# Which queue issues the weight loads: a transformer encoder on one core

## The chip, the cores and the metric

One core of a Trainium2 chip runs the whole kernel. The metric is the device time of one execution in microseconds (us); the kernel before took 2937.95 us, the median of three runs (2937.46 to 2938.80).

The core's engines work side by side and meet through semaphores: TensorE (PE in the profile, PEld its weight loads), VectorE (DVE), ScalarE (ACT), GpSimd (POOL) and SyncE (SP). SP computes nothing: it issues DMA transfers. GpSimd issues DMAs too. Each of the two works through its own list in order, so an instruction that waits holds back those behind it. SP's transfers stand in the profile under queue q1 (hardware_dynamic), GpSimd's under q0 (software_dynamic).

## What is computed

```python
for l in range(2):                                   # 1024 tokens, width 1024, fp32
    h = rms_norm(x, g_mix[l]); proj = h @ w_in[l]
    # A: 6 heads, dense, from a latent space; B: 6 heads, dilated windows; C: 4 heads, 2-D neighbourhood
    qa  = rms_norm(c_q,  q_norm[l])  @ w_uq[l]       # up-projection of the latents
    kva = rms_norm(c_kv, kv_norm[l]) @ w_ukv[l]
    mixed = concat(rms_norm(o_a), rms_norm(o_b), rms_norm(o_c))
    x = x + mixed @ w_out[l]
    h2 = rms_norm(x, g_mlp[l])
    x = x + square(relu(h2 @ w_mlp_in[l])) @ w_mlp_out[l]
return rms_norm(x, g_final)
```

## The kernel before

Tokens are cut into ST = 8 tiles of 128. Every fp32 matrix is split into a high part and the rest, and three matmuls replace one: high by high, high by low, low by high. ACT writes the high part (`split_job`, `split_a`, `hi_up`, `hi_down`), DVE the rest (`rest`, L891).

**Weights** come as units of up to 2048 fp32 numbers per partition (1 MB) in a stream in HBM. A layer has NU = 50 units: two for each of nine jobs (a, bq, up, bk, bv, cqk, cv, o0, o1), then 32 for the feed-forward part. They go through two buffers, `raw[0]` for even and `raw[1]` for odd units. A load adds to `raw_in`; ACT waits for that and copies the high part; DVE then takes the low part and adds to `split_lo`. A load of unit u waits for `split_lo` of unit u - 2 (`load_unit`), since only then its buffer is free. In all there are 102 loads, every one on SP's list.

**Stages of a layer.** (1) Norm of x, tile by tile: ACT squares and sums (L661) and takes the root (L664), DVE scales by it and by the gain gB (L908), TensorE transposes (L1201), ACT and DVE write high and low parts of hT. Each tile's ACT part waits for DVE's part of the tile before. x is parked in HBM, as its place is used for staging. (2) Projections, in the order of the list `EVENTS`, which all engines follow: entries "acc" (the 24, 18 or 6 matmuls of a tile, L1233, four PSUM banks in turn), "turn" (transposes of a staged tile, L1270, high and low parts into `tst`, L777 and L767 on ACT) and "split" (a weight unit). Queries and keys go to HBM as features (`feats`, stored from one of NTS = 3 slots of `tst`, by SP), values as `values` (from one of two slots of `vst`, by GpSimd, L614). ACT waits, before it fills a slot, for the stores that left it. (3) Attention, 16 heads in turn; SP loads features, values and biases, GpSimd the values of the C heads and moves their outputs. (4) Norm, output projection o0 and o1, x back from HBM. (5) Norm and feed-forward part: 16 groups, each an "up" half (L1407) and a "down" half (L1422), one unit each, loaded in a hardware loop (L560).

**SP's list** in order: the rows of x with ident, gB and, after x tiles 3 and 5, the units 0 and 1 (L395); pair, cos, sin. In each layer: gL, units 2 and 3, the park stores of x (L496), gB, units 4 and 5, then `EVENTS`: at each "split" the load of unit u + 2 (L406), at each turn to be stored its feature stores (L515 for "ur", L521 and L526 for "cqk", L532 for the others); then heads; x back, with units 16 and 17 after tile 1; gB; the loop over 32 units; gB; units 0 and 1 of the next layer; the stores of the output.

**GpSimd's list:** memsets (eps is one, L575; ACT waits for it before its first table load), and in each layer the 24 value stores in the order of `EVENTS`, each after DVE's low part; then the C heads' transfers (L587, L597, L605).

Of the kernel before, what the change touches and what calls it, by code (L numbers as in the profile page):

```python
# [52 lines left out]
def unit_len(job, half):  # L53
    if job == "up":
        return (2 * UQ, UKV)[half]
    return KT // 2 * WIDTH[job]
# [162 lines left out]
def encoder(nc, x_in, wstream, gains, lat_gains, cos_in, sin_in, bias_b, bias_c, ident_in, pair_in, out):  # L219
# [69 lines left out]
    with ctx:  # L289
# [43 lines left out]
        def hold(eng):  # L333

            eng.sem_inc(passed, 1)
# [5 lines left out]
        def unit_of(job, half):  # L341
            return 2 * JOBS.index(job) + half
# [42 lines left out]
        def _(sp):  # L385
# [4 lines left out]
            for t in range(1, ST):  # L390
                sp.dma_start(x[:, t, :], x_in[t * P:(t + 1) * P, :]).then_inc(x_loaded[t], 16)
                if t in (3, 5):
                    u = t // 2 - 1
                    length = unit_len("a", u)
                    sp.dma_start(raw[:, u, 0:length], wstream[u, :, 0:length]).then_inc(raw_in[u], 16)  # L395
            sp.dma_start(pair[:, :], pair_in).then_inc(const_in, 16)
            sp.dma_start(cos[:, :, :], cos_in).then_inc(const_in, 16)
            sp.dma_start(sin[:, :, :], sin_in).then_inc(const_in, 16)
            for k in range(2):
                sp.sem_inc(fin_out[k], 16 * (ST // 2))  # L400

            def load_unit(l, u, length=ULEN):

                sp.wait_ge(split_lo, l * NU + u + 1)
                hold(sp)
                sp.dma_start(raw[:, u % 2, 0:length], wstream[l * NU + u, :, 0:length]).then_inc(raw_in[u % 2], 16)  # L406

# [81 lines left out]
            for l in range(DEPTH):  # L489
                sp.dma_start(gL[:, :], lat_gains[l]).then_inc(gl_in, 16)  # L490
                for u in (2, 3):
                    load_unit(l, u, unit_len(JOBS[u // 2], u % 2))

                for t in range(ST):
                    sp.wait_ge(hn_ready, l * N_HN + t + 1)
                    sp.dma_start(x_park[t], x[:, t, :]).then_inc(parked, 16)  # L496
                load_gain(l, 1)
                for u in (4, 5):
                    load_unit(l, u, unit_len(JOBS[u // 2], u % 2))
                turn = vt = 0  # L500
                for e in EVENTS:
                    if e[0] == "acc" and e[1] == "cv":
                        first_head(l, e[2], turn, vt)
                    if e[0] == "split":
                        u = unit_of(e[1], e[2]) + 2
                        load_unit(l, u, unit_len(JOBS[u // 2], u % 2))
                    elif e in STORED:
                        n = TURNS.index(e)
# [39 lines left out]
                for t in range(ST):  # L548
                    sp.wait_ge(hn_ready, l * N_HN + ST + t + 1)
                    sp.dma_start(x[:, t, :], x_park[t]).then_inc(x_loaded[t], 16)  # L550
                    if t == 1:
                        load_unit(l, 16)
                        load_unit(l, 17)
                load_gain(l, 2)
                with sp.Fori(0, NG) as g:
                    load_unit_pair = l * NU + MLP0 + 2 * g
                    for k in range(2):
                        sp.wait_ge(split_lo, load_unit_pair + k + 1)
                        hold(sp)
                        sp.dma_start(raw[:, k, :], wstream[l * NU + MLP0 + 2 * g + k]).then_inc(raw_in[k], 16)  # L560

                load_gain(l, 3)
                for u in range(2):
                    load_unit(l, NU + u, unit_len("a", u))
                for t in range(ST):
# [7 lines left out]
        def _(pool):  # L573

            pool.memset(eps[:, :], EPS).then_inc(eps_set, 1)  # L575

            def load_grid_values(l, n):
# [30 lines left out]
            for l in range(DEPTH):  # L608
                for vt, e in enumerate(VSTAGED):
                    k = vt % 2  # L610
# [19 lines left out]
                park_grid(l, grids[-1])  # L630
                read_grid(l, grids[-1])


# [943 lines left out]
```

## Time and profile before

| | us |
|---|---|
| median of three runs | 2937.95 |
| the profiled execution | 2937.11 |
| its span, first to last instruction | 2935.0 |
| TensorE matmul busy (97%) | 2854.4 |
| VectorE busy (59%) | 1719.8 |
| ScalarE busy (36%) | 1058.0 |
| GpSimd busy (5%) | 141.7 |

Busy times are sums over an engine's instructions; matmuls are pipelined, so their sum says how long TensorE had work, not that it ran at its peak. The span is cut by stages: projections of layer 0 to about 287 us, attention to 650, output projection to 763, feed-forward to 1476; then the same for layer 1. q1 carried 254.16 MB, q0 29.41 MB. An idle stretch of an engine is printed in brackets with what ended it: the "releaser". A releaser with q (DVEq, ACTq) is that engine's sequencer, mostly a semaphore after a drain.

### The profile page before, as it was taken

How to read it: one execution, taken by the hardware profiler on the slowest of the kernel's cores; microseconds unless marked ns; L12 is line 12 of the kernel's file. 1: busy time of each engine (PE TensorE's matmuls, PEld its weight loads, DVE VectorE, ACT ScalarE, POOL GpSimd, SP SyncE). 2: the span in 40 equal slices, each digit the busy share in tenths (PEclk: the TensorE clock that was granted, in tenths of full speed). 3: DMA queues.
4: the chain of work that ended last, by engine and by line, in shares of the span. 5: the costliest groups of instructions: out<-in, count | busy, mean ns of one | idle time of the engine just before them, and what ended most of it. 6: DMA issues, size and time to landing. Idle time of an engine off the chain costs nothing.

```text
span 2935.0 us, 39902 instructions
## 1 busy us (share of the span) xinstructions
PE 2854.4 (97%) x14640; PEld 2439.2 (83%) x14640; DVE 1719.8 (59%) x2998; ACT 1058.0 (36%) x1976; POOL 141.7 (5%) x253
## 2 busy tenths in 40 slices
PE   7999999989999999999999999999899999999998
PEld 7898888878888888888798978888788888888887
DVE  5641777875555455455666337788655455455457
ACT  5332777874311111111244237778632111111113
POOL 0000330000000000000000012300000000000000
PEclk9999999999999999999999999999999999999999
DMA  5656884313111111111146577743221111111111
GB/s 195 183 188 156 199 192 113 88 43 115 43 44 57 43 43 57 43 43 64 45 176 205 168 191 179 178 101 87 67 78 43 43 57 43 43 57 43 43 62 69
DMA packets 182359, 285.34 MB, mean 97 GB/s; under 512 B 48848, under 2 KB 138576, under 8 KB 172496
## 3 DMA queue, kind: packets, MB, share of 16 engines
q1 hardware_dynamic: 171600, 254.16, 29.7%
q0 software_dynamic: 10624, 29.41, 3.6%
q8 instruction: 81, 1.33, 0.2%
q14 instruction: 54, 0.44, 0.1%
HBM read 210.60 MB, written 72.88 MB: 97 GB/s over the span
## 4 chain that ended last, share of the span: by engine, by line
PE 86%; DVE 5%; issue 3%; DMA 3%; ACT 2%; DVEq 1%; SPq 0%; ACTq 0%; POOLq 0%
PE ps L1407 24%; PE ps L1233 20%; PE ps L1422 18%; PE ps L1306 7%; PE ps L1320 6%; PE ps L1352 6%; PE ps L1362 2%; PE ps L1201 1%; DMA biasC<-in_bias_c 1%; DMA values<-vst 1%; PE ps L1270 1%; PE ps L1345 1%; DVE x L1154 1%; DVE hn L908 1%; DVE vbuf L1141 1%
## 5 line engine op out<-in xcount | busy, mean ns | idle before, releaser
L1422 PE MATMUL ps<-w_dn,hid 128*128 128x512 f32 x3072 | 713.6, 391 | 1.4
L1407 PE MATMUL ps<-hT,w_up 128*128 128x512 f32 x3072 | 702.5, 389 | 3.3 <-DVE hT L891 3.3
L1422 PEld LDWEIGHTS ps<-w_dn,hid 128*128 128x128 f32 x3072 | 573.6, 188 | 132.5 <-DVE x L1154 14.0
L1407 PEld LDWEIGHTS ps<-hT,w_up 128*128 128x128 f32 x3072 | 576.2, 188 | 123.1 <-ACT rbuf L841 3.7
L1233 PE MATMUL ps<-ws,hT 128*128 128x384 f32 (+3 forms) x3072 | 607.7, 356 | 3.1 <-issue 1.6
L1233 PEld LDWEIGHTS ps<-ws,hT 128*128 128x128 f32 x3072 | 535.1, 190 | 50.3 <-DVE ws L891 2.7
L1154 DVE TENSOR_TENSOR x<-ps,x 128x512 f32<-128x512 f32 x512 | 342.9, 689 | 223.9 <-PE ps L1422 223.7
L1141 DVE TENSOR_TENSOR vbuf<-rbuf 128x512 f32<-128x512 f32 x128 | 88.6, 692 | 371.0 <-ACT rbuf L841 371.0
L792 ACT ACTIVATE pT<-ps 128x512 fp32r<-128x512 f32 (+1 forms) x448 | 240.5, 582 | 141.5 <-PE ps L1320 139.6
L891 DVE TENSOR_TENSOR pT<-ps,pT 128x512 fp32r<-128x512 f32 (+1 forms) x448 | 281.4, 664 | 6.9 <-ACT pT L792 5.8
L841 ACT ACTIVATE rbuf<-ps 128x512 f32<-128x512 f32 x128 | 76.6, 598 | 553.9 <-PE ps L1407 553.9
L799 ACT ACTIVATE prob<-ps,a_nm 128x1024 f32<-128x1024 f32 (+1 forms) x256 | 252.8, 987 | 35.5 <-DVE a_nm L1056 16.2
L827 ACT ACTIVATE w_dn<-raw 128x2048 fp32r<-128x2048 f32 x32 | 61.3, 1917 | 556.3 <-PE ps L1422 556.3
L1320 PE MATMUL ps<-ident,prob 128*128 128x128 f32 x1728 | 232.2, 273 | 5.9 <-DVE pT L891 3.0
L1306 PE MATMUL ps<-head 128*128 128x512 f32 x768 | 229.6, 400 | 7.1 <-DVEq L1002 5.2
L1320 PEld LDWEIGHTS ps<-ident,prob 128*128 128x128 f32 x1728 | 202.7, 140 | 39.2 <-ACT prob L799 8.3
L1352 PE MATMUL ps<-pT,head 128*128 128x512 f32 x768 | 225.2, 416 | 1.8 <-DVE pT L891 1.8
L1306 PEld LDWEIGHTS ps<-head 128*128 128x128 f32 x768 | 140.4, 190 | 37.1 <-DVEq L1002 6.1
L1352 PEld LDWEIGHTS ps<-pT,head 128*128 128x128 f32 x768 | 131.1, 190 | 20.8 <-DVE pT L891 4.0
L1039 DVE TENSOR_REDUCE a_nm<-ps 128x1 f32<-128x1024 f32 x96 | 117.4, 1223 | 51.1 <-PE ps L1306 48.9
L1044 DVE CUSTOM_DVE_ANT_0 ps<-ps,tabB 128x1024 f32<-128x1024 f32 x96 | 118.1, 1230 | 37.8 <-PE ps L1306 35.8
L1201 PE MATMUL ps<-ident,hn 128*128 128x128 f32 x448 | 70.3, 307 | 40.8 <-DVEq L910 20.5
(85 smaller groups left out, 2140.8 us busy)
## 6 DMA issues: line engine op xcount, KB each, us to landing
raw<-in_wstream SPq DMA_DIRECT2D x76, 1024.0 KB, 4.9
head<-feats SPq DMA_DIRECT2D x192, 256.0 KB, 6.3
feats<-tst SPq DMA_DIRECT2D x128, 192.0 KB, 2.6
values<-vst POOLq DMA_DIRECT2D x32, 384.0 KB, 3.2
head<-values SPq DMA_DIRECT2D x24, 512.0 KB, 4.0
biasC<-in_bias_c SPq DMA_DIRECT2D x16, 768.0 KB, 12.3
raw<-in_wstream SPq DMA_DIRECT2D x12, 768.0 KB, 5.8
x_park<-x SPq DMA_DIRECT2D x16, 512.0 KB, 9.5
```

Of the source, the lines that this page charges most:

```text
L792: act.activation(pT[:, b % 2, HI, k0:k0 + nk, (it % 4) * P:(it % 4 + 1) * P], ps[:, 4 + g % 2, 0:nk * P].rearrange("p (k s) -> p k s", s=P ...
L799: act.activation(probability(i), score(i), ACT.Exp, bias=a_nm[:, i:i + 1], scale=-1.0 if ITEMS[i][0] == "B" else 1.0, accum_out=a_den[:, i ...
L891: return dve.tensor_tensor(out_lo, full, words(hi), ALU.subtract)
L1044: dve.tensor_tensor_reduce(out=score(i), in0=score(i), in1=tabB[:, 896 - P * q:896 - P * q + SEQ], scale=1.0, scalar=-NEG, op0=ALU.add, op ...
L1141: dve.tensor_tensor(vbuf[:, k % 2, :], rbuf[:, k % 2, :], rbuf[:, k % 2, :], ALU.mult)
L1154: dve.tensor_tensor(x[:, s, cols], ps[:, 2 + m % 4, :], x[:, s, cols], ALU.add)\
L1233: last = pe.matmul(out_, a, b, start=(n == 0), stop=(n == len(mms) - 1))
L1306: last = pe.matmul(ps[:, b0 + kh, :], a, b, start=(k == 0), stop=(k == len(mm) - 1))
L1320: last = pe.transpose(ps[:, 4 + g % 2, j * P:(j + 1) * P], probability(i)[:, c:c + P], ident[:, :])
L1352: last = pe.matmul(bank, hb[:, 4096 + kt * P:4096 + (kt + 1) * P], pT[:, b % 2, w, kt, :], start=(part == 0 and kt == 0 and w == 0), stop= ...
L1407: last = pe.matmul(ps[:, k % 2, :], w_up[0 if first else 1][:, w1, kt, ft * P:(ft + 1) * P], hT[:, w2, kt, sh * 512:(sh + 1) * 512], start ...
L1422: last = pe.matmul(ps[:, 2 + m % 4, :], hid[slot][:, w1, ft, s * P:(s + 1) * P], w_dn[1 if last_group else 0][:, w2, ft, nh * 512:(nh + 1) ...
```

## The change

All weight loads leave SP's list and go to GpSimd's, with their waits. SP keeps x, features, head loads, biases, gains, constants and outputs. GpSimd starts with units 0 and 1, ahead of the memset of eps; in each layer it loads units 2 to 5, then walks `EVENTS`: at a "split" it loads unit u + 2, at a value tile it stores the values. After the C heads it loads units 16 and 17, then runs the loop over the 32 feed-forward units, then the next layer's units 0 and 1.

```diff
@@ sync
             for t in range(1, ST):
                 sp.dma_start(x[:, t, :], x_in[t * P:(t + 1) * P, :]).then_inc(x_loaded[t], 16)
-                if t in (3, 5):
-                    u = t // 2 - 1
-                    length = unit_len("a", u)
-                    sp.dma_start(raw[:, u, 0:length], wstream[u, :, 0:length]).then_inc(raw_in[u], 16)
...
-                for u in (2, 3):
-                    load_unit(l, u, unit_len(JOBS[u // 2], u % 2))
...
-                for u in (4, 5):
-                    load_unit(l, u, unit_len(JOBS[u // 2], u % 2))
...
-                    if e[0] == "split":
-                        u = unit_of(e[1], e[2]) + 2
-                        load_unit(l, u, unit_len(JOBS[u // 2], u % 2))
-                    elif e in STORED:
+                    if e in STORED:
...
-                    if t == 1:
-                        load_unit(l, 16)
-                        load_unit(l, 17)
                 load_gain(l, 2)
-                with sp.Fori(0, NG) as g:
...
                 load_gain(l, 3)
-                for u in range(2):
-                    load_unit(l, NU + u, unit_len("a", u))
@@ gpsimd
+            for u in range(2):
+                length = unit_len("a", u)
+                pool.dma_start(raw[:, u, 0:length], wstream[u, :, 0:length]).then_inc(raw_in[u], 16)
             pool.memset(eps[:, :], EPS).then_inc(eps_set, 1)
+
+            def load_unit(l, u, length=ULEN):
+
+                pool.wait_ge(split_lo, l * NU + u + 1)
+                hold(pool)
+                pool.dma_start(raw[:, u % 2, 0:length], wstream[l * NU + u, :, 0:length]).then_inc(raw_in[u % 2], 16)
...
             for l in range(DEPTH):
-                for vt, e in enumerate(VSTAGED):
+                for u in range(2, 6):
+                    load_unit(l, u, unit_len(JOBS[u // 2], u % 2))
+                for e in EVENTS:
+                    if e[0] == "split":
+                        u = unit_of(e[1], e[2]) + 2
+                        load_unit(l, u, unit_len(JOBS[u // 2], u % 2))
+                    if e not in VSTAGED:
+                        continue
+                    vt = VSTAGED.index(e)
                     k = vt % 2
                     pool.wait_ge(acc_free_dve, l * DVE_FREE_N + frees_before(ACCS.index(e) + 1, False))
...
                 read_grid(l, grids[-1])
+                for u in (16, 17):
+                    load_unit(l, u)
+                with pool.Fori(0, NG) as g:
+                    load_unit_pair = l * NU + MLP0 + 2 * g
+                    for k in range(2):
+                        pool.wait_ge(split_lo, load_unit_pair + k + 1)
+                        hold(pool)
+                        pool.dma_start(raw[:, k, :], wstream[l * NU + MLP0 + 2 * g + k]).then_inc(raw_in[k], 16)
+                for u in range(2):
+                    load_unit(l, NU + u, unit_len("a", u))
```

## Rows read from the trace of the kernel before

**Rows 1.** The page, busy us, share of the span and instructions.

```profile
PE 2854.4 (97%) x14640; PEld 2439.2 (83%) x14640; DVE 1719.8 (59%) x2998; ACT 1058.0 (36%) x1976; POOL 141.7 (5%) x253
```

**Rows 2.** Timeline of PE: start, us, instruction [idle before it <-releaser].

```profile
7.73 1.94 PE L1201 MATMUL ps<-ident,hn 128*128 128x128 f32 x8 [7.73 <-DVEq L910]
...
118.73 0.69 PE L1270 MATMUL ps<-ident,stage 128*128 128x128 f32 x2 [2.72 <-DVE tst L891]
...
125.57 0.52 PE L1270 MATMUL ps<-ident,stage 128*128 128x128 f32 x3 [2.42 <-ACTq L735]
...
129.27 2.36 PE L1233 MATMUL ps<-ws,hT 128*128 128x384 f32 x12 [0.77 <-DVE ws L891]
...
1571.95 0.52 PE L1270 MATMUL ps<-ident,stage 128*128 128x128 f32 x3 [1.67 <-ACTq L735]
...
1575.65 2.36 PE L1233 MATMUL ps<-ws,hT 128*128 128x384 f32 x12 [0.75 <-DVE ws L891]
```

**Rows 3.** The tile raw: who waited, us, times; then its loads' landing.

```profile
  ACT ws L647: 1.1, 2
...
DMA to landing us min/median/max: 3.6/4.9/12.6
```

**Rows 4.** Timeline of SP's queue, the start.

```profile
3.63 0.45 SPq L395 DMA_DIRECT2D raw<-in_wstream  x1
...
24.51 8.70 SPq L406 DMA_DIRECT2D raw<-in_wstream  x2
```

**Rows 5.** Timeline of ACT, the start.

```profile
4.45 1.06 ACT L661 ACTIVATE hn<-x 128x1024 f32<-128x1024 f32 x1 [2.21 <-DMA x<-in_x]
...
7.92 1.06 ACT L661 ACTIVATE hn<-x 128x1024 f32<-128x1024 f32 x1 [1.96 <-DMA x<-in_x]
...
11.14 1.06 ACT L661 ACTIVATE hn<-x 128x1024 f32<-128x1024 f32 x1 [0.73 <-DVEq L910]
```

**Rows 6.** Windows: us, busy us by engine, granted clock, DMA share, GB/s.

```profile
4.00:6.00 2.00, 0.00 (x0) 0.00 (x0) 0.00 (x0) 1.44 (x3) 0.00 (x0) 1.00 1.02 367
...
14.00:16.00 2.00, 0.84 (x4) 0.87 (x5) 1.53 (x4) 1.85 (x4) 0.00 (x0) 1.00 1.02 428
```

**Rows 7.** GpSimd's value stores: ns min/median/max; us from issue to landing.

```profile
L614 POOL DMA_DIRECT2D values<-vst x48: 542/542/738, 107.0 to 1736.9; - x48
...
DMA to landing us min/median/max: 2.6/3.3/8.2
```

**Rows 8.** The two DMA queues in 277.5 to 279.1 us: packets, MB, share.

```profile
q1 hardware_dynamic: 98, 0.33, 64.8%
q0 software_dynamic: 70, 0.22, 39.9%
```

**Rows 9.** The chain that ended last: start, us, piece; then page's DMA issues.

```profile
119.11 5.13 DMA feats<-tst
...
1566.12 4.50 DMA feats<-tst
...
feats<-tst SPq DMA_DIRECT2D x128, 192.0 KB, 2.6
```

**Rows 10.** Timeline of SP's queue before the first of these stores.

```profile
116.82 0.35 SPq L406 DMA_DIRECT2D raw<-in_wstream  x1
118.70 4.33 SPq L532 DMA_DIRECT2D feats<-tst  x6
```

**Rows 11.** Windows at the two stores (columns as in rows 6).

```profile
120.00:122.00 2.00, 2.00 (x10) 2.00 (x9) 0.06 (x1) 0.00 (x0) 0.00 (x0) 0.63 0.90 310
...
1565.00:1569.00 4.00, 3.26 (x12) 3.25 (x13) 2.05 (x5) 1.36 (x3) 0.00 (x0) 0.57 0.99 287
```

**Rows 12.** Timelines of SP's queue and ACT in the value projection.

```profile
195.78 2.55 SPq L406 DMA_DIRECT2D raw<-in_wstream  x2
...
204.18 0.49 ACT L743 ACTIVATE vst<-ps 128x384 fp32r<-128x384 f32 x1 [4.29 <-DMA values<-vst]
```

**Rows 13.** Timelines of ACT and SP's queue, a group of the feed-forward part.

```profile
1008.30 1.92 ACT L827 ACTIVATE w_dn<-raw 128x2048 fp32r<-128x2048 f32 x1 [19.86 <-PE ps L1422]
...
1012.78 22.48 SPq L560 DMA_DIRECT2D raw<-in_wstream  x2
```

More of the change, by code:

```diff
@@ L400, in _ @@
                 sp.sem_inc(fin_out[k], 16 * (ST // 2))
[L402 to L406, printed above, removed]
             def load_gain(l, k):
@@ L550, in _ @@
                     sp.dma_start(x[:, t, :], x_park[t]).then_inc(x_loaded[t], 16)
-                    if t == 1:
-                        load_unit(l, 16)
-                        load_unit(l, 17)
                 load_gain(l, 2)
-                with sp.Fori(0, NG) as g:
[L556 to L560, printed above, removed]
                 load_gain(l, 3)
-                for u in range(2):
-                    load_unit(l, NU + u, unit_len("a", u))
                 for t in range(ST):
```

## Prediction

> **What bounds the kernel now.** I read the busy times first. TensorE's matmuls cover 97% of the span, and VectorE, the next, 59% [rows 1]. So the change can gain or lose only where TensorE stands still for something a transfer delivers. Next I read its timeline for pauses, in order of time. Two places matter here [rows 2]. At the start it waits 7.73 us for its first operand, and shorter times before the next five sets of transposes. In the latent up-projection of layer 0 it pauses 2.72, 2.42 and 0.77 us near 118 to 129 us; layer 1 has the same three, the last two at 1571.95 and 1575.65 us with 1.67 and 0.75 us. The feed-forward stage, where 64 of the 102 weight loads are, has no pause that a weight load ends.
>
> The list of who waited for the tile `raw` says the same from the other side: of all the converting copies that read it, ACT waited for the transfer twice, 1.1 us in all [rows 3]. Loading weights sooner is thus worth nothing by itself. What the change can alter is what travels beside the weights: the rows of x at the start, the feature stores (which lose the weights ahead of them in SP's queue) and the value stores (which get them ahead in GpSimd's).
>
> **The start.** Now SP issues x tile 0, the identity, gB, x tiles 1 to 3, weight unit 0, x 4 and 5, unit 1, x 6 and 7 [rows 4]. ACT waits 2.21 us for x tile 0 and starts at 4.45, waits 1.96 us for tile 1 and starts at 7.92; from then on it waits for DVE, not for a transfer: tile 2 follows at 11.14, 3.2 us on [rows 5]. That is a serial chain (ACT's square and root, DVE's scaling, ACT again), so what x tile 1 loses, everything behind it loses. From 4 to 16 us the DMA engines are full, at 367 GB/s in the first 2 us slice of that and 428 in the last [rows 6].
>
> After the change GpSimd issues both units, 832 KB each (1.70 MB), as its first work. It has nothing before them but the memsets of the first microsecond, and a DMA costs it 0.54 us, its first one 0.74 [rows 7]. The bytes then run beside SP's queue from about 2.3 us, as SP's own first bytes do. How two queues share the engines shows in one window, where the value store on GpSimd's queue and 4 KB rows on SP's were both moving: 70 packets of one and 98 of the other, shares of 39.9% and 64.8% [rows 8]. Neither had the way to itself. Up to tile 1's landing SP's queue carries x 0, 64 KB, gB and x 1, 1.64 MB, about as much as the two units. If the queues alternate row by row, the 16 rows per engine of the two units are all served before the 24 rows per engine of x 0, gB and x 1 are done. Tile 1 then lands later by the whole time of the units: 1.70 MB at 410 GB/s (my estimate between the slices of [rows 6]) = 4.1 us. It would land near 12.0 instead of 7.9. Tile 0 would slip by about 2 us and gB, which DVE needs for tile 0, to about 10.4; both lie inside the same 4.1 us, since tile 1 would come no sooner than that anyway. Tiles 2 to 7 were needed at 11.14 and later and now have 4.1 us more; their bytes end where they ended before, near 20 us. The delayed memset of eps (1.3 us) only moves ACT's table load, which lies in the 2.21 us wait. Bounds: zero if SP's queue were served first or GpSimd's first DMA came late, 4.1 at the top, because there are no more bytes to be overtaken by. I take **+4.1**, the end that the near-equal shares of the shared window speak for. Nothing later gives this back: from its first projection to 118 us TensorE has no pause to absorb it.
>
> Two edits on SP's list go with it. Park stores of x no longer wait behind units 2 and 3 (24.51 for the first of the two [rows 4]); they go out earlier, and TensorE runs through that stretch, so this is worth 0. Those units come no later than now.
>
> **The feature stores.** In both layers the chain of the end runs through one feature store: issued at 118.70 it lands after 5.13 us, and in layer 1 after 4.50 us, while the median of such stores is 2.6 [rows 9]. SP had issued a 768 KB weight load 1.9 us before it (116.82 [rows 10]; layer 1 has the same order). In one queue the store waits for the rest of it. With the load in GpSimd's queue the store starts at once but shares: I estimate that it is done about 1 us sooner. Bounds: nothing (the DMA engines are nearly full there, 0.90 and 0.99 busy [rows 11], and the same bytes must move), and 2.5 and 1.9 us if the store took its median. ACT waits for that store, TensorE for ACT (the 2.42 and 1.67 us pauses), so it is on the path. I take **-1.0 in each layer, -2.0 in all**. The 2.72 us pause ahead of it is set by ACT's and DVE's order of work and stays. Later waits for feature stores repeat with no load near them and stay.
>
> **What GpSimd's queue takes on.** Each load but the first two waits for a low half that DVE writes in the order of the same list as the value stores, so no store is held by a load's wait; a load's issue costs a store 0.5 us. The one tight spot is the value projection: units of cv are loaded at 195.78, and ACT, whose copy at 204.18 needs the third value store landed, waited 4.29 us for it already [rows 12]. Queued behind 2 x 512 KB it may land 1 to 2 us later. But that copy frees one of four banks, and TensorE, which takes 2.36 us for half a tile of 24 matmuls [rows 2], wants it back three tiles on, 12 us or more later: 0. In the feed-forward loop a load leaves at 1012.78, and its buffer, read at 1008.30 [rows 13], is read again one group later, near 1052 (two loads, one for each half of a group, span 22.48 us from the first's start to the second's end, so a group takes some 44 us); landing takes 4.9 us [rows 3], so some 34 us of cover. It covers GpSimd's issue, its loop and any wait of GpSimd for DVE: 0. At the layers' joint the next bq units come sooner, and with that the 1.1 us that ACT waited for them [rows 3]; TensorE is not waiting there: 0. Units 16 and 17 no longer follow x's first two reloads: 0.
>
> **Clock.** TensorE's granted clock fell to half for short stretches after pauses (0.63 of full in 120 to 122 us, 0.57 in 1565 to 1569 us [rows 11]). A shift of 4 us can move such a stretch onto more or fewer matmuls. TensorE was busy all 2.0 us of the first at 0.63, where 1.3 us of full clock would have done, so one such shift is worth about 1 us either way; with a handful of places I allow 2 us each way, centred on 0.
>
> **Sum.** The profiled run took 2937.11 us for a span of 2935.0, 0.84 under the median of the three runs. On the run: 2937.11 + 4.1 - 2.0 = 2939.2. On the median: 2937.95 + 2.1 = **2940.0**.
>
> **Rivals.**
> *Only the order changes, no store gets faster.* The DMA engines are full around the two stores, so the weight bytes may delay a store as much from a second queue as from the same one. Then only the start counts: 2937.95 + 4.1 = 2942.0. For it: the busy share of 0.90 to 0.99; against: the load was issued first and its bytes stand wholly ahead now. The Trainium skill, page "DMA: Bandwidth & Descriptors", section "Issuing engines are not separate DMA queues", says that transfers started on several engines run on the same 16 DMA engines and that spreading them saves only the time of issuing. By that rule this rival is the outcome; the long landings behind a weight load speak against it, as a queue's order seems to count there.
>
> *The start costs nothing.* GpSimd's first DMA is slow to begin, or SP's queue goes first. Then x tile 1 lands as before and only the stores gain: 2936.0. For it: no row shows how long GpSimd's first DMA takes to begin; against: value stores of 384 KB land in 2.6 us at best, issue to end [rows 7], and there are over 5 us before tile 1 is in.
>
> *The pauses vanish whole.* If the stores take their median and the half-clock stretch goes as well, each layer saves up to 2.42 + 0.77 and 1.67 + 0.75 us plus 1 us of clock, 7.6 in all; with no loss at the start 2930.4.
>
> *Slower: value stores stall behind weights.* Place: the eight value stores of the bv projection in each layer, with two staging buffers, behind the cqk and cv units in one queue. The price starts when a store lands more than about 12 us late, for then ACT cannot free a bank in time. A value store that did wait among other traffic took 8.2 us at most [rows 7]. If GpSimd's queue moved 1 MB in 15 us and not in 3 (70 GB/s), one stall of 5 us per layer would follow: 2937.95 + 4.1 + 10 = 2952. A value store of 384 KB that lands 2.6 us after its issue moved at 150 GB/s or more, so I hold it unlikely.
>
> **Chances.** Forecast 0.50; no store gain 0.20; no start cost 0.15; pauses vanish whole 0.05; slower by stalls 0.07; none of these 0.03. What this kernel's measurement can tell from no change is about 0.2%, 5.9 us: under 2932.1 or over 2943.8. Faster is the case of the vanished pauses and a bit: 0.06. Slower is the stall case and the top end of the first two with the clock against them (+4.1 + 2): 0.14. Same: 0.80. The range takes the first three cases with 1 to 2 us of clock on either side and a little of the slow tail: 2934.5 to 2945.0.
>
> **What would show each step.** Start: ACT's square of x tile 1 at about 12.0 instead of 7.92, tile 0's near 6.4, all that follows later by as much. Stores: landing of the chain's store at 4 instead of 5.13 us, TensorE's pause of 2.42 down to about 1.4. GpSimd: 102 DMAs more, of some 0.55 us each. Feed-forward: same pauses as before. I would be wrong if x tile 1 kept its time, if a pause on raw or on vst appeared in TensorE's list, or if the feed-forward's pace of 44 us per group changed.

## The result

| | median us (lowest to highest) | runs |
|---|---|---|
| before | 2938.99 (2935.04 to 2943.01) | 20 |
| after | 2943.39 (2939.32 to 2946.27) | 20 |

The ratio after to before is 1.0015, with a 95% interval of 1.0008 to 1.0021: slower by 4.4 us, between 2.4 and 6.2. The forecast of 2940.0 lay 3.4 us under the median, its range held it, and the change is within the 0.2% that was called "same"; but the interval leaves no doubt about the sign. The profiled execution of after took 2939.32 us (span 2937.6), the fastest of its 20, and 2.2 us more than the profiled one of before. So a sum over the two traces must come to 2.2, and what the medians show beyond it is to be looked for in the experiments. One execution of e5 (3957.0 us) and one of before beside e5, e7, e8 and e9 (3242.1 us) were slow; the ratios leave them out.

The page of after, with busy times as in [rows 1], then the DMA queues (packets, MB, share) and the commonest weight load (KB, us to landing):

```profile
PE 2852.4 (97%) x14640; PEld 2437.9 (83%) x14640; DVE 1718.7 (59%) x2998; ACT 1056.9 (36%) x1976; POOL 195.6 (7%) x355
...
q1 hardware_dynamic: 156912, 155.85, 20.0%
q0 software_dynamic: 25184, 127.72, 13.5%
...
raw<-in_wstream POOLq DMA_DIRECT2D x76, 1024.0 KB, 5.1
```

GpSimd has 102 instructions more than in [rows 1], for 53.9 us, 0.53 us each; no other engine's work changed by more than its scatter. The loads are on q0 now, 98.3 MB of them.

TensorE's timeline, the lines that answer to [rows 2], and one that has no counterpart there:

```profile
10.64 1.94 PE L1198 MATMUL ps<-ident,hn 128*128 128x128 f32 x8 [10.64 <-DVEq L907]
...
122.60 0.44 PE L1267 MATMUL ps<-ident,stage 128*128 128x128 f32 x2 [2.72 <-DVE tst L888]
...
128.96 0.52 PE L1267 MATMUL ps<-ident,stage 128*128 128x128 f32 x3 [1.60 <-ACTq L732]
...
132.66 2.38 PE L1230 MATMUL ps<-ws,hT 128*128 128x384 f32 x12 [0.77 <-DVE ws L888]
...
1469.40 1.16 PE L1198 MATMUL ps<-ident,hn 128*128 128x128 f32 x8 [2.08 <-DVE hT L888]
...
1576.79 0.52 PE L1267 MATMUL ps<-ident,stage 128*128 128x128 f32 x3 [1.58 <-ACTq L732]
1580.49 2.38 PE L1230 MATMUL ps<-ws,hT 128*128 128x384 f32 x12 [0.77 <-DVE ws L888]
```

Read as differences to [rows 2], this list is much of the ledger. The first operand comes 2.91 us later, and the pause at 122.60 stands 3.87 us later than before's at 118.73. The pause for a feature store has shrunk from 2.42 to 1.60 us: behind it, after is 3.39 us late. Only 0.48 of the 0.82 us came through, since the clock behind the first pause was low for longer: 0.88, 0.50 and 0.77 in the three stretches of 2 us from 122 to 128 us, which come to some 3.4 us at the lower level; in before it was some 2.7 us, from the pause's end at 118.73 on (0.63 in 120 to 122, 1.00 after that). In layer 1 the same pause went from 1.67 to 1.58 only. And at 1469.40, in the first norm of layer 1, TensorE waits 2.08 us where before had no pause: 4.84 us behind at 1576.79 (before: 1571.95).

The rest of the ledger has no line in this list. TensorE starts 14640 matmuls in each trace, so the lag can be read at every one of them. It falls from 3.41 us near 165 us to 2.30 near 180, since before has a pause of 0.90 us there that after lacks; more on it below. It grows from 2.30 to 2.80 us through the feed-forward part. Behind 1735 us it goes from 5.41 to 3.25 us, and to 2.64 at the end. Half of that is a difference in clock. TensorE waited 3.03 us at 1762.34 in before and 2.40 us at 1767.06 in after, each time for DVE, in the attention of layer 1. These are windows of before and of after behind that wait, columns as in [rows 6]:

```profile
1764.00:1768.00 4.00, 4.00 (x17) 3.41 (x16) 2.30 (x6) 2.46 (x7) 0.00 (x0) 0.66 1.03 219
```

```profile
1768.00:1772.00 4.00, 4.00 (x26) 3.48 (x25) 3.26 (x10) 3.45 (x9) 0.00 (x0) 1.00 1.06 223
```

At a granted clock of 0.66, the 4.00 us are work for 2.6 us at full clock. That is 1.4 us which before lost there and after did not. No kernel here moves this place on purpose, so I put it down to scatter and not to the change.

ACT's timeline of after, which answers to [rows 5], with its third norm tile of layer 1:

```profile
4.60 1.06 ACT L658 ACTIVATE hn<-x 128x1024 f32<-128x1024 f32 x1 [1.67 <-DMA x<-in_x]
...
11.91 1.06 ACT L658 ACTIVATE hn<-x 128x1024 f32<-128x1024 f32 x1 [5.79 <-DMA x<-in_x]
...
15.11 1.06 ACT L658 ACTIVATE hn<-x 128x1024 f32<-128x1024 f32 x1 [0.72 <-DVEq L907]
...
1465.38 1.06 ACT L658 ACTIVATE hn<-x 128x1024 f32<-128x1024 f32 x1 [3.51 <-DMA out<-hn]
```

x tile 1 is squared at 11.91 and not 7.92, tile 2 follows 3.2 us on as before. The queues in 4 to 10 us of after (packets, MB, share), while GpSimd's two units were moving:

```profile
q0 software_dynamic: 245, 1.52, 65.8%
q1 hardware_dynamic: 306, 0.83, 36.1%
```

GpSimd's queue moved almost twice the bytes of SP's. Its two loads landed 6.7 and 9.7 us after their issue at 1.38 and 2.06, so both were in by 11.8 us, just before tile 1.

The last line of ACT's timeline is the new pause's cause. The square writes `hn`, which has two slots, and waits for a store that still reads the slot of the first tile: `out<-hn`, issued by SP (each norm tile here is stored to `out` as well). The chain that ended last has it in one piece:

```profile
1459.31 5.91 DMA out<-hn
```

Who issued what there, and at the start, stands in the timelines of GpSimd and of SP's queue:

```profile
1.38 1.21 POOL L547 DMA_DIRECT2D raw<-in_wstream  x2 [0.81 <-POOLq L1566]
...
1455.41 0.53 POOL L554 DMA_DIRECT2D raw<-in_wstream  x1 [22.00 <-DVE ws L888]
1458.40 0.53 POOL L554 DMA_DIRECT2D raw<-in_wstream  x1 [2.47 <-DVE ws L888]
```

```profile
1459.31 28.88 SPq L537 DMA_DIRECT2D out<-hn  x8
```

Before, layer 1's units 2 and 3 stood on SP's list behind these eight stores (and gL) and left at 1484.02. On GpSimd nothing is ahead of them but their own waits: they leave at 1455.41 and 1458.40, just before the first store. The landing times of the 16 stores of `out`, min, median and max, are 2.6/2.6/3.8 us before and these after:

```profile
DMA to landing us min/median/max: 2.6/2.6/5.9
```

In the chain that ended last, the feature stores that answer to [rows 9]; then the queues in 122.9 to 127.7 us, the stretch of the first (packets, MB, share), and one window of 440 us in the feed-forward part, columns as in [rows 6]:

```profile
122.98 4.65 DMA feats<-tst
...
1570.85 4.62 DMA feats<-tst
```

```profile
q1 hardware_dynamic: 1458, 0.72, 50.1%
q0 software_dynamic: 134, 0.73, 45.8%
```

```profile
960.00:1400.00 440.00, 439.55 (x1926) 360.48 (x1925) 224.59 (x301) 61.17 (x60) 10.58 (x20) 1.00 0.14 48
```

Both queues move together and take about half of the engines' time each, nearer to halves than in [rows 8]. In these 440 us of the feed-forward stage TensorE is busy for 439.55 us, and it was for the same 439.55 us before. Matmul by matmul, after still falls back by 0.33 us there. That is not GpSimd's list: e8, with no load of this stage on it, falls back as much, and e1, with all of them on it, does not.

### The profile page after: what moved, and what is told of

Read it like the earlier page. It is cut to its first block, busy times and chain, and to the rows that moved or that the text cites. A ratio compares the mean times of both kernels' runs of the same rounds, so it can differ in the third digit from the quotient of the medians.

```text
span 2937.6 us, 39902 instructions
## 1 busy us (share of the span) xinstructions
PE 2852.4 (97%) x14640; PEld 2437.9 (83%) x14640; DVE 1718.7 (59%) x2998; ACT 1056.9 (36%) x1976; POOL 195.6 (7%) x355
## 4 chain that ended last, share of the span: by engine, by line
PE 89%; DVE 3%; DMA 3%; issue 2%; ACT 2%; DVEq 1%; SPq 0%; ACTq 0%; POOLq 0%
PE ps L1404 24%; PE ps L1419 21%; PE ps L1230 20%; PE ps L1303 7%; PE ps L1317 6%; PE ps L1349 6%; PE ps L1359 2%; PE ps L1198 1%; PE ps L1267 1%; DMA biasC<-in_bias_c 1%; DMA values<-vst 1%; PE ps L1342 1%; DVE hn L905 1%; PE ps L1294 1%; DVE ws L888 0%
## 5 line engine op out<-in xcount | busy, mean ns | idle before, releaser
L626 POOL DMA_DIRECT2D raw<-in_wstream x64 | 33.8, 529 | 1408.1 <-DVE w_up L888 779.5
```

## Experiments

In the kernels that split the loads between the two lists, a function `on_pool(l, u)` says which list issues a unit, and each buffer has a landing semaphore for each queue, so that ACT waits for the right one. All else is before's code, with GpSimd's list as in after where it has loads. "Lag" is measured at the sixth set of transposes, 26.80 us in before and 30.78 in after. With nothing of GpSimd in front, the executions profiled for before, e1, e3, e5, e6, e7, e9, e10 and e12 put ACT's square of x tile 1 at 7.92 (before) to 9.14 us (e7), and the sixth transposes at 26.80 (before) to 28.00 us (e7). So single readings of the start carry some 0.6 us either way, and before's was the earliest of the nine. The ratios below have intervals of 0.0009 to 0.0010 (2.6 to 3 us) to either side, and each run has one trace.

### The start alone, and after without it

e2 gives GpSimd the units 0 and 1 of layer 0 and nothing else; e1 is after with these two back on SP.

```diff
+        def on_pool(l, u):            # e2
+            return l == 0 and u < 2
...
+            return l > 0 or u > 1     # e1
```

> The kernel before, with only units 0 and 1 issued by GpSimd at the start. Theory: x tile 1's square at 11.8 to 12.0 us, everything later by 4.0 us to the end, +4 us; no pause at the joint, the pauses near 118 and 125 us as in the kernel before (2.72 and 2.42 us). Rival (the start's delay is given back later): +0 to +1 us at the end though the first tiles are 4 us late.

> The change, but with weight units 0 and 1 back on SP's list, behind x tiles 3 and 5; all other loads stay on GpSimd's queue. Theory (the time went at two places: the start, 4.0 us, and the joint of the layers, 2.0 us, with some 1 us won back at the feature stores): ACT's square of x tile 1 starts near 7.9 again, TensorE's sixth set of transposes near 26.8, and the pause of 2 us at the joint stays; about +1 us against the kernel before. Rival (the cost is spread over a hundred loads by GpSimd's queue, and the start is made up for later): the time stays about 4 us over the kernel before. Rival (the start is all): 0 to -1 us.

Measured: e2 2943.59 us against 2938.97, ratio 1.0016 (1.0007 to 1.0025), the whole loss of after with 2 of its 102 loads. e1 2939.38, ratio 0.9999 (0.9990 to 1.0008). ACT's timeline of e2:

```profile
4.48 1.06 ACT L707 ACTIVATE hn<-x 128x1024 f32<-128x1024 f32 x1 [1.58 <-DMA x<-in_x]
12.06 1.06 ACT L707 ACTIVATE hn<-x 128x1024 f32<-128x1024 f32 x1 [6.06 <-DMA x<-in_x]
```

The sixth transposes start at 30.93 us, 4.13 late. In e1 tile 1's square is at 8.73 us. e2 has no pause at the joint of the layers (0.21 us there), e1 keeps it; TensorE's timeline of e1:

```profile
1465.69 1.16 PE L1248 MATMUL ps<-ident,hn 128*128 128x128 f32 x8 [2.01 <-DVE hT L938]
```

So the loss at the start comes from the two units, and the pause at the joint from other loads.

### The same loads on GpSimd, but after x tile 1

e5 is after with the memset of eps first and a wait for x tile 1 ahead of the two units.

```diff
+            pool.memset(eps[:, :], EPS).then_inc(eps_set, 1)
+            pool.wait_ge(x_loaded[1], 16)
             for u in range(2):
...
-            pool.memset(eps[:, :], EPS).then_inc(eps_set, 1)
```

> The change, but GpSimd sets eps first and then waits until x tile 1 has landed before it issues units 0 and 1. Both stay on GpSimd's queue. Theory (the start's 4 us are the bytes put in front of x tile 1, not the queue they come from): tile 1's square near 8 us, the sixth set of transposes near 27 us; units 0 and 1 are in before ACT reads the first near 21 us; about 4 us faster than the change, +0 to +1 us against the kernel before. Rival (GpSimd's queue itself makes the start slow): the first transposes stay some 3 to 4 us late.

Measured: 2939.52 us against 2938.97, 1.0002 (0.9993 to 1.0011). ACT's timeline:

```profile
8.38 1.06 ACT L659 ACTIVATE hn<-x 128x1024 f32<-128x1024 f32 x1 [2.33 <-DMA x<-in_x]
```

The sixth transposes are at 27.25. The queue is the same as in after, the bytes are the same, only their time differs: what costs 3.5 to 4 us is not GpSimd's issue or its list, but bytes that run in front of tile 1.

### Half of the bytes, and more of them

e11 gives GpSimd unit 0 alone (832 KB); e8 is e2 with both loads at their full 2048 numbers per partition (2.10 MB in place of 1.70).

```diff
+            return l == 0 and u == 0      # e11
...
-                length = unit_len("a", u)
+                length = ULEN                 # e8, GpSimd's start only
```

> The kernel before with unit 0 alone issued by GpSimd at the start, unit 1 left on SP's list behind x tile 5: half the bytes in front of x tile 1. Theory (shift in proportion to the bytes): tile 1's square near 10.3 us, half way between 8.5 (nothing in front) and 12.06 (both units), +2 us at the end. Rival (a fixed cost of two queues): near 12 us, +4 us. Rival (unit 0 alone hides behind gB): near 8.5, 0 us.

> The kernel before with units 0 and 1 issued by GpSimd at the start, and each of them loaded at full length (8192 bytes per partition instead of 6656, 2.10 MB and not 1.70). The bytes beyond the unit are not used. Theory (x tile 1 comes later by the time of all bytes put beside it): the shift of 4.0 us becomes 4.0 x 8192/6656 = 4.9 us; tile 1's square near 12.9, the sixth set of transposes near 31.7, +5 us. Rival (a fixed cost of GpSimd's first transfers): the same shift as with the shorter units, +4.0 us, the sixth set near 30.8.

Measured, e11: 2938.00 us against 2937.21, 1.0002 (0.9993 to 1.0011). e8: 2944.06 against 2938.97, 1.0020 (1.0011 to 1.0030). ACT's timelines, e11 and then e8:

```profile
9.84 1.06 ACT L707 ACTIVATE hn<-x 128x1024 f32<-128x1024 f32 x1 [3.86 <-DVEq L957]
```

```profile
12.47 1.06 ACT L707 ACTIVATE hn<-x 128x1024 f32<-128x1024 f32 x1 [6.56 <-DMA x<-in_x]
```

With one unit, 0.85 MB / 410 GB/s = 2.1 us are in front (an estimate by the rate that the prediction took), and the sixth transposes stand at 28.71, 1.9 us behind before's. Against the eight other traces with nothing in front it is 0.7 (e7) to 1.5 us. ACT does not even wait for tile 1: it waits for DVE's scaling of tile 0, which waits for gB, and gB is in at 8.18 us. e7 waits in the same way without any load of GpSimd's, with gB in at 7.48. So half the bytes cost between a fifth and a half of the whole, and by its ratio e11 alone could not be told from before. With 0.4 MB more, all of it in front would add 1.0 us; the square of tile 1 moved by 0.2 to 0.6 us against e2, e4 (12.23) and after. Both units of e8 were in by 12.2 us, before tile 1, so the bytes were all in front; what they cost was less than their share. e8 and e11 agree with the price growing with the bytes, but not with its being in proportion to them.

### The joint of the layers

e4 is after with one wait more: in layer 1 GpSimd holds units 2 and 3 until DVE has scaled the eighth tile of the first norm, near where SP's order had them. e9 adds e1's edit to it.

```diff
+                if l:
+                    pool.wait_ge(hn_ready, (l - 1) * N_HN + 4 * ST)
+                    hold(pool)
                 for u in range(2, 6):
                     load_unit(l, u, unit_len(JOBS[u // 2], u % 2))
```

> The change, with one wait more: GpSimd loads units 2 and 3 of layer 1 only when the last tile of layer 0's last norm is scaled, as SP's list did. Theory (these loads share the DMA engines with the output stores that ACT waits for): the pause of 2.08 us before the transposes near 1469 us is gone, ACT no longer waits for an output store, about 2 us faster than the change, +2.4 us against the kernel before. Rival (that pause is chance or comes from something else): the pause and +4.4 us stay.

> The change with units 0 and 1 back on SP's list and the loads of layer 1's units 2 and 3 held until the last norm of layer 0 is scaled; the other 98 loads stay on GpSimd's queue. Theory (start and joint are the two losses, the rest costs nothing and wins a little): no late start, no pause at the joint; 0 to -1.5 us against the kernel before. Rival (the queue of 98 loads has a cost of its own): +1 us or more although both places are mended.

Measured: e4 2942.57 us against 2938.97, 1.0009 (1.0000 to 1.0019); e9 2937.69, 0.9995 (0.9986 to 1.0004). TensorE's timeline of e4 at the joint:

```profile
1461.58 1.09 PE L1201 MATMUL ps<-ident,hn 128*128 128x128 f32 x8 [1.61 <-DVEq L910]
1465.64 1.16 PE L1201 MATMUL ps<-ident,hn 128*128 128x128 f32 x8 [0.21 <-DVE hT L891]
```

There is no pause of 2 us behind these, and no wait of ACT for `out` in e4 or e9; after, e1 and e5, in which the units leave beside the stores, all have both (2.08, 2.01 and 1.94 us). Of the traces with those units on SP (before, e2, e3, e6, e7, e8, e10, e11, e12) none has it. The cause is shown: it is the loads that leave beside these stores. Its price by the ratios is 1.2 us (e1 over e9, 0.0004), 1.8 us (after over e4, 0.0006) or 2.1 us (e5 over e9, 0.0007), each with an interval that holds zero; the traces say 2.0.

### The feature stores: which queue

e3 moves only the loads of the projection stages' list (units 6 to 15), and so takes the weights out of SP's queue at the two stores, with no effect on start or joint.

```diff
+            return 6 <= u < 16
```

> The kernel before, with only the loads of units 6 to 15 (those issued between feature stores) moved to GpSimd's queue; start, joint and feed-forward stay on SP. Theory: the pause of 2.42 us near 125 us falls to 1.6 and that of 1.67 us in layer 1 to about 1.6, start and joint as before; -0.5 to -1 us. Rival (two queues are as slow as one, the shorter pause was chance): pauses as in the kernel before, 0 us.

Measured: 2937.58 us against 2938.97, 0.9996 (0.9987 to 1.0005). The same readings from all kernels, landing of the chain's store and TensorE's pause behind it:

| weight load of the turn | layer 0: landing, pause | layer 1: landing, pause |
|---|---|---|
| on SP: before | 5.13, 2.42 | 4.50, 1.67 |
| e2 | 5.22, 2.44 | 7.21, 5.73 |
| e6 | 5.06, 2.02 | 7.27, 5.78 |
| e8 | 5.41, 2.37 | 5.37, 3.90 |
| e11 | 4.92, 0.88 | 7.49, 4.67 |
| on GpSimd: after | 4.65, 1.60 | 4.62, 1.58 |
| e1 | 4.86, 1.83 | 4.25, 1.23 |
| e3 | 4.51, 1.48 | 5.45, 3.95 |
| e4 | 4.80, 1.75 | 5.68, 2.87 |
| e5 | 4.40, 1.37 | 4.88, 1.85 |
| e9 | 4.47, 1.42 | 5.52, 4.02 |

The means of the pauses are 2.03 and 4.35 us with the load on SP, 1.58 and 2.58 on GpSimd. In layer 0 the gain is 0.5 us, and all six landings on GpSimd are below the five on SP. The pauses alone can mislead, since the one of 0.77 us behind it is gone in some traces; the time from the same matmul before the pause to the same one 16 us on says 0.6 us.

In layer 1 the means are not a fair comparison, and the traces hold what goes with the scatter. The profile has queues of the kind "instruction" beside q0 and q1. One of them, q8, moves a packet of 16 KB every 10 to 25 us in the projections, which takes 0.9 us or more on its DMA engine. In layer 1 it falls close to the store, before or after its issue:

| landing | weight load on SP | weight load on GpSimd | q8's packet starts |
|---|---|---|---|
| 4.25 to 4.88 | before | after, e1, e5 | 2.6 to 4.8 us before the store |
| 5.37 to 5.68 | e8 | e3, e4, e9 | 2.1 to 2.9 us after it |
| 7.21 to 7.49 | e2, e6, e11 | none | 4.4 to 4.7 us after it |

In the last two rows the store lands 2.8 to 3.3 us after the packet's start, in all seven traces. q8's packet in e2, in 1572 to 1573 us, and the window behind it, in which the DMA engines are nearly idle and the store is not in yet:

```profile
q8 instruction: 1, 0.02, 5.5%
```

```profile
1573.00:1574.40 1.40, 0.00 (x0) 0.00 (x0) 0.00 (x0) 0.00 (x0) 0.00 (x0) 0.50 0.15 39
```

Within a row the two lists are alike: TensorE's way from before the pause to 46 us on took, against before, 0.1, -0.1 and 0.9 us more in after, e1 and e5; 2.4 in e8 and 2.4 to 2.8 in e3, e4 and e9; 3.2 to 3.8 in e2, e6 and e11. So no gain of GpSimd's list is to be seen in layer 1 once the packet's place is the same. Near 165 us of layer 0 the same shows again. In before, e4, e6 and e11 the packet comes 3.8 us sooner against TensorE's work than in after, e1, e2, e3, e5, e8 and e9, and these four lose 1.1 us there by a pause of 0.9 that the other seven do not have, whichever list loads.

No run here moved the packet, so that it holds the store up is argued from its place and not shown; nor is it known what sets the place, or whether GpSimd's list keeps the last row away. It does mean that before's trace, on which the forecast rested, showed layer 1 at its best.

### The feature stores: no load beside them at all

e7 keeps all loads on SP but takes the two bv units out of the place ahead of the store: they are issued at the sixth and seventh tile of the queries' up-projection. e10 cuts each into four quarters of 192 KB, one per tile from the fourth to the seventh, the first unit beside the queries' tiles and the second beside the keys'. e12 is e10 again, on another chip.

```diff
+                    for half in range(2):                               # e7
+                        if e == ("acc", "uq", 5 + half):
+                            load_unit(l, unit_of("bv", half), unit_len("bv", half))
+                    if e[0] == "split" and e[1] != "bk":
...
+                    for half, kind in enumerate(("uq", "uk")):          # e10, e12
+                        if e[0:2] == ("acc", kind) and 3 <= e[2] < 7:
+                            u, n = unit_of("bv", half), unit_len("bv", half) // 4
+                            c = n * (e[2] - 3)
...
+                            sp.dma_start(raw[:, half, c:c + n], wstream[l * NU + u, :, c:c + n])\
+                              .then_inc(raw_in[0][half], 16)
```

> The kernel before with all loads on SP, but the two bv units loaded later in SP's list, at the sixth and seventh tile of the up-projection, and not at the splits of bk beside the feature store of the chain. Theory (that store is late by the weight load before it, on whichever queue): it lands in 2.6 to 3.5 us, not 5.13, the pause of 2.42 near 125 us falls below 1 us, the one of 1.67 us in layer 1 as well; about -2 to -3 us. Rival (the store is late for its own reasons, the many stores after it or its read): it still takes about 4.5 to 5 us and the pauses stay within 0.5 us, 0 us.

> The kernel before with all loads on SP, the two bv units not loaded at the splits of bk but in four quarters of 192 KB each, one quarter at each of the tiles 3 to 6 of the up-projection, so that no feature store has more than a quarter beside it. Theory (a whole unit beside a store costs 2 us wherever it stands, since the store waits for all of its bytes; the stage has about 0.5 us to spare in each tile): the pauses near 125 us and 1572 us fall below 0.5 us as in the run with the late loads, and no new pause of 1.6 to 2.1 us comes up; -2 to -3 us. Rival (the stage is short of DMA time as a whole, so the bytes cost the same in any size): new pauses that sum to 2 us and more in each layer, 0 to +3 us.

> The same kernel as e10_bv_pieces once more, to narrow its interval (0.9994 [0.9985, 1.0003]). Theory (a whole unit beside the feature stores costs 0.7 us in layer 0 and 2 to 4 us in layer 1 of most runs, a quarter next to nothing): again 2 us or more under the kernel before, pauses near 123 and 1571 us at 1.2 us or less, while the kernel before has 2.4 and 1.7 to 5.8 us there. Rival (it was chance): a ratio of 1.000 or more.

Measured: e7 2942.42 us against 2938.97, 1.0013 (1.0004 to 1.0022); e10 2935.53 against 2937.21, 0.9994 (0.9985 to 1.0003); e12 2936.72 against 2939.89, 0.9995 (0.9986 to 1.0004). The chain's store in e7, then TensorE's timeline of e7:

```profile
120.23 2.36 DMA feats<-tst
```

```profile
152.12 0.52 PE L1320 MATMUL ps<-ident,stage 128*128 128x128 f32 x3 [1.60 <-ACTq L784]
...
1573.72 0.52 PE L1320 MATMUL ps<-ident,stage 128*128 128x128 f32 x3 [0.21 <-ACTq L784]
...
1602.46 0.52 PE L1320 MATMUL ps<-ident,stage 128*128 128x128 f32 x3 [2.14 <-ACTq L784]
1613.17 0.52 PE L1320 MATMUL ps<-ident,stage 128*128 128x128 f32 x3 [2.05 <-ACTq L784]
```

In layer 0 a store with no weights near it lands in 2.36 us (2.37 in e10 and e12). It takes 4.9 to 5.4 us behind a load in its own queue and 4.4 to 4.9 beside one in the other queue, in the mean 5.15 and 4.62. So a load costs the store most of its time from either side; leaving its queue gives back only 0.5 of 2.8 us. In layer 1 the store took 4.25, 3.94 and 3.96 us in e7, e10 and e12 with no load ahead of it, so there a good part of its time isn't the load's; q8's packet came 0.6 to 1.2 us after it in these three. And e7 shows that moving the load in time pays the price elsewhere: the pause near 125 us is gone and the one near 1573 is down to 0.21 us, but new ones of 1.60, 2.14 and 2.05 us stand where the loads now meet other stores of the same staging slots. It was expected to win 2 to 3 us, and it is slower than before by 3.8.

In quarters, at most 192 KB of weights are issued just before a store. TensorE's timeline of e10:

```profile
123.25 0.52 PE L1326 MATMUL ps<-ident,stage 128*128 128x128 f32 x3 [0.90 <-ACTq L790]
...
1570.76 0.52 PE L1326 MATMUL ps<-ident,stage 128*128 128x128 f32 x3 [1.19 <-ACTq L790]
```

Against [rows 2] that is 2.42 down to 0.90 and 1.67 down to 1.19, where less than 0.5 was expected, with 0.65 and 0.59 us new behind them in layer 1. e12, the same kernel, has no such pause in layer 0 and 2.48 us in layer 1, with 0.98 us new behind it. Both comparisons point to a gain of 1.5 to 1.8 us, less than the 2 to 3 us expected, and both intervals hold 1. These are the lowest ratios with e9's and e3's, and none of them is shown to beat before.

### The feed-forward loads alone

e6 moves only the units of the feed-forward part, 64 of the 102.

```diff
+            return u >= MLP0
```

> The kernel before with only the 64 loads of the feed-forward stages moved to GpSimd's queue. Theory (34 us of cover for a load of 5 us): 0 us, within 0.1% of the kernel before, the same pauses of TensorE in both feed-forward stages, a group of 44 us as before. Rival (GpSimd's queue costs something per load): 64 times any cost that reaches TensorE, +1 us or more.

Measured: 2939.55 us against 2937.21, ratio 1.0002 (0.9993 to 1.0011). The window of the loop is TensorE's 439.55 us once more:

```profile
960.00:1400.00 440.00, 439.55 (x1926) 360.40 (x1925) 224.61 (x301) 61.14 (x60) 10.62 (x20) 1.00 0.14 48
```

No cost of the 64 loads' move is seen, though the interval reaches to 3.2 us. The medians differ by 2.3 us and the ratio says 0.6; what e6's trace has more than before's is no part of this stage: its pause at layer 1's store was 5.78 us, with before's list at that place.

## Why the prediction was right, and where it was not

**The start: right.** Forecast +4.1 us, x tile 1's square near 12.0. It came at 11.91, the lag is 3.98 in after and 4.13 in e2 against before, but before's trace was the earliest: against the other eight with nothing in front (27.18 to 28.00) after's lag is 2.8 to 3.6. The ratio of e2 makes it 4.7. The mechanism, bytes of the second queue that all stand in front of tile 1, is borne out by e5 (same queue, later: no lag) and by the landings, both units in by 11.8 us and tile 1 squared at 11.91; e11 and e8 support it only weakly. Three details were off. The bytes were to run beside SP's from 2.3 us; q0 moved none before 3.5 us, though GpSimd's first DMA left at 1.38. So tile 0, which was to slip by 2 us to 6.4, was squared at 4.60. The shares read from [rows 8] as nearly equal came out as 65.8% to 36.1%; what the estimate needed, all of the units in before tile 1, held. And the first transposes came at 10.64 us, 2.91 late and not 4, since only gB was held. Neither mattered: as the prediction said, both lie inside tile 1's delay.

**The feature stores: the mechanism seen in layer 0, the size too large, and nothing seen in layer 1.** Forecast -1.0 us in each layer, a landing of 4 us and a pause of 1.4. Layer 0: landing 4.65, pause 1.60, gain 0.82. Layer 1: landing 4.62 where before had 4.50, pause 1.58, gain 0.09. Over eleven traces the pause in layer 0 is 0.5 us shorter, and in layer 1 the lists are alike once traces with q8's packet at the same place are compared; by the ratios e3 and e9 gain 1.2 and 1.5 us, intervals to zero and beyond. Two steps failed. One is that layer 1 was priced from one landing of 4.50 us as if it were the load's: without any load it was 3.94 to 4.25. The other is smaller. The store was taken to start at once and share for a short while. The two queues shared from end to end of that stretch, 50.1% and 45.8% of the DMA time. The rival in which no store gets faster, and with it the rule of the Trainium skill (page "DMA: Bandwidth & Descriptors", section "Issuing engines are not separate DMA queues"), is nearer to this than the prediction allowed: in layer 0 most of the delay stays when the load is on the other engine's queue (4.4 to 4.9 us against 2.36 alone). By the rule alone nothing would be gained; the 0.5 us of layer 0 say that order within a queue counts a little, and there the measurement decides.

**The joint of the layers: wrong, the term that was missed.** The prediction wrote: "the next bq units come sooner, and with that the 1.1 us that ACT waited for them; TensorE is not waiting there: 0". Both halves are true: those waits of ACT are gone. But it asked only who needs the units, not what moves beside them. SP's order had kept them behind eight stores of `out`; GpSimd's let them go 26 to 29 us earlier, onto the first of the stores, whose slot ACT needs back for the third tile. Issued at 1459.31, that store landed 5.91 us later, at 1465.2, and ACT's square began at 1465.38; the longest landing before was 3.8. TensorE paused for 2.08. That is +2.0 us (e4 and e9 take it away, e1 and e5 keep it). The rows that would have told it were there: SP's timeline at the joint, and the norm as a serial chain, which the start had just been costed by.

**Value stores and feed-forward: right.** No pause of TensorE is ended by a value store; ACT's waits for `vst` sum to 38.9 us over 10, before 38.0 over 10. TensorE's busy time in the window of the feed-forward stage is the same to the hundredth, and e6 agrees. The stall rival did not come: weight loads land after 5.1 us at the median, not 15.

**The sum.** For the profiled pair: +3.98 at the start, -0.11 up to the first store, -0.48 over it, -1.1 near 168 us, +0.5 up to the joint, +2.0 at the joint and +0.1 at layer 1's store = +4.9; the trace is 4.84 behind at 1576.79. Then 2.2 us go away, 1.4 of them by a stretch of low clock that only before had, and the spans end 2.6 us apart, the times 2.2. So the small difference of the two traces is in good part luck: -1.1 and -2.2 us stand at places that the change was not seen to touch. Over the runs, 3.5 to 4.0 at the start, +2.0 at the joint and -0.5 in layer 0 make +5.0 to +5.5, against 4.4 (2.4 to 6.2) measured; if GpSimd's list does keep the late packet away, it is less. The forecast's +2.1 lacked the joint's +2.0 and had 1.0 to 1.5 us too much gain at the stores. Its range caught the result through the clock's allowance, which is the right result for a reason that was not its own. The parts by ratios agree within their intervals: start alone +4.7 us (e2), all but the start -0.3 (e1), start and stores without the joint +2.6 (e4), stores alone -1.2 (e3), loads moved without start and joint -1.5 (e9).

**Clock.** Behind the same pauses TensorE's granted clock fell in after too: 0.50, the lower of its two levels (1.2 and 2.4 GHz), in 124 to 126 us, and 0.60 in the mean of 1570 to 1574, as 0.63 and 0.57 in [rows 11]. The prediction's allowance of 2 us either way was needed: the stretch near 1765 us alone was worth 1.4, and 0.3 of layer 0's shorter pause went in the same way. It was not a cost of the change as far as is known.

## What to carry over

When a list is cut in two, look not only at who waits for the moved transfers but at what the old order kept apart: every transfer that may now leave earlier will do so, and it runs beside the one that somebody needs. Here two loads out of 102 cost some four microseconds because they overtook the first rows of x, two more cost two microseconds because they overtook a store whose buffer was wanted back, and one wait or two lines left on the old list took either away. If a queue must be relieved, keep that order with a wait, and do not expect much: a store beside a load is late on either list. Smaller pieces looked a little better here and were not shown to be. And one trace is one draw: the same store behind the same load took 4.50 us in one and 7.49 in another, so read such a wait from several traces before you price it.

## What the runs showed of the hardware

- Two queues, two rates of landing: GpSimd's 1 MB load takes 0.53 us of its time to issue and lands in 5.1 us at the median, SP's took 0.33 us for the issue in the feed-forward loop and landed in 4.9 us.
- GpSimd's first DMA left only at 1.38 us, 0.8 us after its memsets, and cost 0.68 us where later ones cost 0.53. Its queue moved nothing until 3.5 us.
- Packets of some 500 B on SP's queue and of some 5 KB on GpSimd's took nearly equal shares of the engines' time for equal bytes (0.72 MB at 50.1%, 0.73 MB at 45.8%), with 1458 packets against 134. With larger packets on both, at the start, GpSimd's queue moved 1.52 MB and SP's 0.83.
- The same store behind the same load on SP landed in 4.50, 5.37, 7.21, 7.27 and 7.49 us in five executions of layer 1, and in 4.92 to 5.41 us in layer 0. The order of the five goes with the place of q8's packet of 16 KB, from 4.1 us before the store to 4.7 us after it. That it is the cause is not shown.
- Behind that packet the DMA engines were 0.15 busy for 1.4 us in e2 while a store was under way.
